# Attention steps joined into rounds of 512 keys, in a kernel of three transformer layers

## The reference, cut to what matters

```python
# layer 1: differential attention (4 heads, 2 maps each) and NSA (8 heads, 3 branches)
a = p[:, :, 0] - lam * p[:, :, 1]          # p: causal softmax of q.k, head width 64
o_diff = einsum(a, v)                       # v is 128 wide, then rms_norm of each head
pc = masked_softmax(q.kc); ps = ...(q.ks); pw = ...(q.kw)
o_nsa = g0 * (pc @ vc) + g1 * (ps @ vs) + g2 * (pw @ vw)
x = x + rms_norm(concat(o_diff, o_nsa) @ w_out); x = x + rms_norm(swiglu(rms_norm(x)))
# layer 2: short convolution and forgetting attention (8 heads)
s = q.k * scale + (c[t] - c[s]);  s = where(causal, s, -inf)   # c: running sum of log f
y_b = softmax(s) @ v
x = x + rms_norm(concat(y_a, y_b) @ w_out); x = x + rms_norm(swiglu(...))
# layer 3: conformer convolution, then the same
```

## Time and profile before

| | |
|---|---|
| median of 3 runs | 1925.96 us (1925.32 to 1926.47) |
| profiled execution | 1925.33 us, of which the span from first to last instruction 1923.5 us |
| PE busy | 1882.1 us, 98% of the span |
| PEld, DVE, ACT, POOL busy | 79%, 42%, 23%, 64% |
| mean granted TensorE clock | 0.988 of full |
| DMA | 168.29 MB, 87 GB/s |

### The profile page before, as it was taken

The page is one execution under the profiler, slowest core; times in us unless marked ns, Lnnn a source line. Parts: engine busy times, 40 slices in busy tenths (PEclk is TensorE's granted clock), DMA queues, the critical chain, the costliest instruction groups (busy, mean ns, idle before and its releaser), DMA issues.

```text
span 1923.5 us, 25700 instructions
## 1 busy us (share of the span) xinstructions
PE 1882.1 (98%) x9410; PEld 1510.2 (79%) x9410; DVE 814.2 (42%) x1397; ACT 437.0 (23%) x902; POOL 1238.6 (64%) x747
## 2 busy tenths in 40 slices
PE   8999999999999999999999999999999999999997
PEld 6776668888888898766878888889787888888886
DVE  5266563643332035154543334004993464334103
ACT  3335672311110022032311111003334331111000
POOL 7964655866666658563786667556657586666662
PEclk9999999999999999999999999999999999999998
DMA  5430102223233214211233333221323223333311
GB/s 206 121 92 30 34 23 77 84 91 98 88 117 106 82 55 144 87 56 44 77 110 94 91 98 116 95 84 50 108 73 99 77 88 90 96 98 108 106 61 44
DMA packets 44879, 168.29 MB, mean 87 GB/s; under 512 B 4984, under 2 KB 7288, under 8 KB 44672
## 3 DMA queue, kind: packets, MB, share of 16 engines
q1 hardware_dynamic: 44496, 164.56, 27.5%
q10 hardware_dynamic: 304, 2.64, 0.4%
HBM read 165.07 MB, written 2.11 MB: 87 GB/s over the span
## 4 chain that ended last, share of the span: by engine, by line
PE 88%; POOL 4%; DVE 4%; issue 2%; ACT 0%; DMA 0%; POOLq 0%; SPq 0%; DVEq 0%
PE psum L554 27%; PE psum L555 26%; PE psum L556 26%; POOL w_lo L443 2%; PE psum L747 2%; PE psum L760 1%; DVE h_lo L1484 1%; DVE tmp L1526 1%; POOL w_hi L440 1%; PE psum L783 1%; PE psum L604 1%; PE psum L851 1%; PE psum L872 1%; POOL x L464 1%; PE psum L612 1%
## 5 line engine op out<-in xcount | busy, mean ns | idle before, releaser
L443 POOL TENSOR_TENSOR w_lo<-raw,w_hi 128x1024 fp32r<-128x1024 f32 (+1 forms) x286 | 748.4, 2617 | 23.8
L554 PE MATMUL psum<-h_hi,w_hi 128*128 128x512 f32 (+1 forms) x1744 | 669.3, 384 | 15.9 <-POOL w_lo L443 9.6
L555 PE MATMUL psum<-h_lo,w_hi 128*128 128x512 f32 (+1 forms) x1744 | 658.3, 377 | 0.0
L556 PE MATMUL psum<-h_hi,w_lo 128*128 128x512 f32 (+1 forms) x1744 | 658.0, 377 | 0.0
L440 POOL TENSOR_SCALAR w_hi<-raw 128x1024 fp32r<-128x1024 f32 (+1 forms) x286 | 322.2, 1127 | 472.5 <-PE psum L556 448.5
L554 PEld LDWEIGHTS psum<-h_hi,w_hi 128*128 128x128 f32 x1744 | 328.6, 188 | 93.6 <-issue 20.8
L556 PEld LDWEIGHTS psum<-h_hi,w_lo 128*128 128x128 f32 x1744 | 327.8, 188 | 67.9
L555 PEld LDWEIGHTS psum<-h_lo,w_hi 128*128 128x128 f32 x1744 | 328.3, 188 | 63.8 <-issue 0.2
L554 PE MATMUL psum<-g_hi,w_hi 128*128 128x512 f32 (+1 forms) x594 | 219.3, 369 | 0.0
L555 PE MATMUL psum<-g_lo,w_hi 128*128 128x512 f32 (+1 forms) x594 | 218.8, 368 | 0.0
L556 PE MATMUL psum<-g_hi,w_lo 128*128 128x512 f32 (+1 forms) x594 | 218.7, 368 | 0.0
(11 more groups left out here) (281 smaller groups left out, 1912.3 us busy)
## 6 DMA issues: line engine op xcount, KB each, us to landing
raw<-in_wide SPq DMA_DIRECT2D x239, 512.0 KB, 3.6
raw<-in_down SPq DMA_DIRECT2D x48, 704.0 KB, 4.0
decay<-decay_rows ACTq DMA_DIRECT2D x1, 2048.0 KB, 7.8
out<-x SPq DMA_DIRECT2D x16, 128.0 KB, 1.7
x<-in_xt SPq DMA_DIRECT2D x3, 512.0 KB, 6.9
x<-in_xt ACTq DMA_DIRECT2D x1, 512.0 KB, 4.5
angles<-in_angles SPq DMA_DIRECT2D x1, 512.0 KB, 10.3
cols<-in_cols SPq DMA_DIRECT2D x1, 221.0 KB, 4.3
```

The costliest lines, as they stand in the source:

```text
L443: nc.gpsimd.tensor_tensor(w_lo[:, slot, 0:w], raw[:, j % RAW, 0:w], w_hi[:, slot, 0:w].bitcast(F32), ALU.subtract).then_inc(units_split, 1)
L554: pe.matmul(out_ap, lhs[0], rhs[0], start=first, stop=False)
L555: pe.matmul(out_ap, lhs[0], rhs[1], start=False, stop=False)
L556: return pe.matmul(out_ap, lhs[1], rhs[0], start=False, stop=last)
```

## The change

- `A_ROUNDS` replaces `STEPS`, `FOX_ROUNDS` replaces `FOX_STEPS`. A round holds one or two steps that lie side by side in the banks: i = 3 alone (512 keys), i = 0 beside i = 2 (128 + 384), and i = 1 beside another i = 1 (256 + 256, of the other branch in NSA, of the next pair in layer 2; alone in the differential attention). Layer 1 has 32 rounds (20 NSA, 12 differential), layer 2 has 10.
- On PE a round t is now turn(t-2), scores(t), mix(t-3). Before it was scores(t), turn(t-3), mix(t-4).
- DVE copies its half of every NSA and layer 2 round, at the head of its round, and it computes the coefficients of round t at the end of round t, one reciprocal and one product for both steps. Before it did this for step t-1 behind the maxima of step t.
- In layer 2 the masks are written first and the scores added to them.
- The weaving: 28 rounds in the eight units of layer 1, four (or two) to a unit; in layer 2 two rounds in each of the first four units and one in each of the last five. POOL now weighs all rounds of a unit before the next split.
- The read of a finished bank in layer 2 moves: `FOX_ENDS` lets ACT and DVE read both banks of two pairs at round r + 4, while PE's mix(5), the first of the third pair, is in round 8, which is just that round.
- In the token compression `low_tokens(1)` moves ahead of the second rotary embedding.

```diff
-STEPS = nsa_steps(0) + nsa_steps(1) + diff_steps(0) + nsa_steps(2) + diff_steps(1) + nsa_steps(3, (1,)) + diff_steps(2) + nsa_steps(3, (2,)) + diff_steps(3)
+def diff_rounds(head):
+    return [[("diff", head, 0, 3)], [("diff", head, 0, 0), ("diff", head, 0, 2)], [("diff", head, 0, 1)]]
+def nsa_rounds(head):
+    return [[("nsa", head, 1, 3)], [("nsa", head, 2, 3)], [("nsa", head, 1, 0), ("nsa", head, 1, 2)],
+            [("nsa", head, 2, 0), ("nsa", head, 2, 2)], [("nsa", head, 1, 1), ("nsa", head, 2, 1)]]
+A_ROUNDS = nsa_rounds(0) + nsa_rounds(1) + diff_rounds(0) + nsa_rounds(2) + diff_rounds(1) + nsa_rounds(3)[:3] + diff_rounds(2) \
+    + nsa_rounds(3)[3:] + diff_rounds(3)
-A_WEAVE = [(3, 5, 6, 7)] + [(1, 3, 4, 6, 7)] * 3 + [(1, 2, 3, 5, 6, 7)] * 3 + [(1, 3, 4, 6, 7)]
-PAIR_TURN, PAIR_MIX = 3, 4
+A_WEAVE = [(5, 7)] + [(1, 3, 5, 7)] * 6 + [(3, 7)]
+ROUND_TURN, ROUND_MIX = 2, 3
...
-WEAVE = [(3, 7)] * 3 + [(2, 5, 7)] + [(3, 7)] * 4 + [(2, 5, 7)]
+FOX_ROUNDS = [r for c in (0, 2) for r in ([(c, 3)], [(c, 0), (c, 2)], [(c + 1, 3)], [(c + 1, 0), (c + 1, 2)], [(c, 1), (c + 1, 1)])]
+FOX_ENDS = (4, 9)
+WEAVE = [(3, 7)] * 4 + [(5,)] * 5
...
+            def pair_round(t, low_start):
+                if 0 <= t - ROUND_TURN < len(A_ROUNDS):
+                    pair_turn(t - ROUND_TURN)
+                if t < len(A_ROUNDS):
+                    pair_scores(t)
+                if 0 <= t - ROUND_MIX < len(A_ROUNDS):
+                    pair_mix(t - ROUND_MIX, low_start)
...
+            def fox_mix(r):
+                steps = FOX_ROUNDS[r]
+                fox_copied(r + 1)
+                if r in (5, 7):
+                    pe.wait_ge(h_low, n.base["h_low"] + (1 if r == 5 else 2))
...
             rope("kc", place_vc)
             add_positions(0)
             add_positions(1)
-            rope("nq0", lambda: low_tokens(0))
-            rope("nq1", lambda: low_tokens(1))
-            for name in ("nq2", "nq3", "ks"):
+            rope_parts("nq0")
+            low_tokens(0)
+            low_tokens(1)
+            rope_sum("nq0")
+            for name in ("nq1", "nq2", "nq3", "ks"):
                 rope(name)
```

More of the change, by code:

```diff
@@ new lines, with places @@
+SET_BEGINS = {key: min(r for r, steps in enumerate(A_ROUNDS) if steps[0][:2] == key) for key in MIX_BANK}
+SET_ENDS = sorted((max(r for r, steps in enumerate(A_ROUNDS) if steps[0][:2] == key),) + key for key in MIX_BANK)
+A_WEAVE = [(5, 7)] + [(1, 3, 5, 7)] * 6 + [(3, 7)]
+A_WOVEN_ROUNDS = [[sum(map(len, A_WEAVE[:j])) + k for k in range(len(A_WEAVE[j]))] for j in range(len(A_WOVEN))]
+A_LEFT = sum(map(len, A_WEAVE))
+ROUND_TURN, ROUND_MIX = 2, 3
+def places(steps):
+    return [sum(step[-1] + 1 for step in steps[:k]) * P for k in range(len(steps))]
@@ new lines, in width, with steps_upto, round_col, step_col @@
+def width(steps):
+    return sum(step[-1] + 1 for step in steps) * P
+def steps_upto(rounds, r):
+    return sum(map(len, rounds[:r]))
+def round_col(r):
+    kind, head, b, i = A_ROUNDS[r][0]
+    if kind == "diff":
+        return 16 * 4 + 8 * head + 2 * i
+    return 16 * head + 2 * steps_upto(nsa_rounds(head), nsa_rounds(head).index(A_ROUNDS[r]))
+def step_col(r, k):
+    return round_col(r) + (2 * k if A_ROUNDS[r][0][0] == "nsa" else 2 * (A_ROUNDS[r][k][3] - A_ROUNDS[r][0][3]))
+def combined_by_dve(r):
+    return A_ROUNDS[r][0][0] == "diff" and A_ROUNDS[r][0][3] == NB - 1
@@ L158, in done_before @@
 def done_before(kind, head):
-    place = next(j for j, end in enumerate(SET_ENDS) if end[1:] == (kind, head))
-    earlier = [end for end in SET_ENDS[:place] if MIX_BANK[end[1:]] == MIX_BANK[kind, head]]
+    earlier = [end for end in SET_ENDS if MIX_BANK[end[1:]] == MIX_BANK[kind, head] and end[0] < SET_BEGINS[kind, head]]
     return earlier[-1][1:] if earlier else None
 def copies_by_dve(upto):
-    return sum(step[0] == "nsa" and step[3] not in COPIED_BY_ACT for step in STEPS[:upto])
-FOX_STEPS = [(c, i) for c in range(4) for i in reversed(range(NB))]
@@ new lines, in pair_scores @@
+            def pair_scores(r):
+                steps = A_ROUNDS[r]
+                if r:
+                    pe.wait_ge(pair_maxed, 2 * steps_upto(A_ROUNDS, r))
+                else:
+                    pe.wait_ge(v_out, len(TOKEN_MAJOR))
+                if steps[0][0] == "diff" and steps[0][3] == NB - 1:
+                    pe.wait_ge(rope_added, ROPES.index(f"dk{steps[0][1]}") + 1)
+                for step, off in zip(steps, places(steps)):
+                    for m in range(2):
+                        mm = pe.matmul(psum[:, 2 + m, off:off + (step[3] + 1) * P], pair_query(step, m), pair_keys(step, m), start=True, stop=True)
+                mm.then_inc(pair_scored, 1)
@@ new lines, in fox_turn, with fox_scores @@
+            def fox_turn(r):
+                pe.wait_ge(fox_weighed, r + 1)
+                if r:
+                    fox_copied(r)
+                for p in range(0, width(FOX_ROUNDS[r]), P):
+                    for m in range(2):
+                        mm = pe.transpose(psum[:, 4 + m, p:p + P], e_fox[:, m, r % 4, p:p + P], ident)
+                mm.then_inc(fox_transposed, 1)
+            def fox_scores(r, first):
+                steps = FOX_ROUNDS[r]
+                if r:
+                    pe.wait_ge(fox_maxed, 2 * steps_upto(FOX_ROUNDS, r))
+                else:
+                    pe.wait_ge(evacuated, n.now("group", -1))
+                    pe.wait_ge(fox_values, NB)
+                for k, (step, off) in enumerate(zip(steps, places(steps))):
+                    diagonal = slice(off + step[1] * P, off + (step[1] + 1) * P)
+                    for m in range(2):
+                        pe.matmul(psum[:, fox_bank(first, m), diagonal], ident16[:], causal16[:], start=k == 0, stop=False, skip_group_check=True)
+                for step, off in zip(steps, places(steps)):
+                    c, i = step
@@ L870, in fox_step @@
+                mm.then_inc(fox_scored, 1)
+            def fox_mix(r):
+                steps = FOX_ROUNDS[r]
+                fox_copied(r + 1)
+                if r in (5, 7):
+                    pe.wait_ge(h_low, n.base["h_low"] + (1 if r == 5 else 2))
+                for step, off in zip(steps, places(steps)):
+                    c, i = step
                     for j in range(i + 1):
```

480 lines of the change are left out of this document (229 added, 251 removed).

## The result

The changed kernel takes 1931.24 us (median of 8 runs, 1929.01 to 1933.53) beside 1925.49 us for the kernel before (8 runs, 1921.77 to 1926.47). The ratio is 1.0033, 95% interval 1.0022 to 1.0043: slower by 5.8 us, where the prediction had 1928.5 us and called a slower kernel the second likeliest. The profiled execution took 1932.91 us (span 1931.0), so it lies 1.7 us above the median.

What follows compares the result with a forecast made beforehand. PE, busy 98% of the span, was taken as the bound. The terms -12 - 4.1 + 8 + 4.3 + 3.8 + 2.6 + 1.5 - 1.2 = +2.9 us gave 1928.5 us, range 1920 to 1937.

Steps and rivals of the forecast that it cites:

- the forecast's own case: Whole kernel: the summed terms hold, giving 1928.5 us, within 1922 to 1930; chance 0.42.
- The likeliest sign, no change: Whole kernel: same time as before had chance 0.42, slower 0.36, faster 0.22; a timing can tell 0.2%, 3.9 us.
- rivals 1 and 2: Faster, 1918 us: layer 1's predicted waits don't appear (0.22). Slower, 1938 us: DVE becomes the bound of layer 1 (0.14).
- Part 1: Layer 1 on PE: fewer, joined rounds save fixed costs beyond the columns; gain 12 us (11 to 13.5).
- Part 2: Layer 2 on PE: fixed costs fall and 0.4 us comes back at the end; gain 4.1 us (3.5 to 4.7).
- Part 3: Layer 1's woven part: PE waits for a round's chain through the other engines; loss 8 us (3 to 12).
- Part 4: Layer 1 behind the last unit: turns wait, the opening starts at E+26.0 for 21.8; loss 4.3 us (2 to 7).
- Part 5: Layer 2, round 8: the third pair's mixing waits for a bank ACT and DVE read; loss 3.8 us (3.4 to 4.2).
- Part 6: PE's clock halves behind waits: loss 2.6 us in layer 2, 1.5 more (0 to 3.4) behind layer 1's last unit.
- the third rival: Layer 1: the clock falls at two more places, 2 * 2 us more, 1932.5 us; chance 0.16.
- Part 7: Token compression: PE's 2.51 us wait for `low_tokens(1)` goes, then PE waits for POOL's splits; gain 1.2 us (0 to 3.5).
- joined steps: Rival, layer 1: joined steps no cheaper than single ones, each joint 0.3 instead of 0.05, 1932.5 us; chance 0.06.

Runs made afterwards that it cites:

- three_coef_late: `three_rounds` plus, in layer 1, DVE's coefficients of round t - 1 behind the maxima of round t and POOL weighing a unit's last round with the next unit's: 1916.69 us.
- three_rounds: The changed kernel, but in layer 1 the turn stands three rounds behind the scores and the mixing four, instead of 2 and 3: 1925.78 us.
- two_coef_late: The changed kernel with its two rounds between scores and turn, but layer 1's coefficients of round t - 1 behind the maxima of round t: 1968.00 us.
- tail_weighed_first: The changed kernel, but POOL weighs rounds 26 to 31 of layer 1 before output-projection splits 35 and 36: 1938.03 us.
- both_mended: The changed kernel with layer 1's three rounds and late coefficients, as in `three_coef_late`, and layer 2's finished banks read at the head of the round: 1910.14 us.
- fox_read_first: The changed kernel, but in layer 2 ACT and DVE read the finished banks at the head of round r + 4 instead of its end: 1924.65 us.

## Why the prediction came out as it did

The time lies in the range (1920 to 1937), 2.7 us above the forecast and just outside the forecast's own case (1922 to 1930). As a change it is twice what was forecast: 5.8 us for 2.9. The likeliest sign, no change, was wrong; slower had 0.36. The range was also said to take in most of rivals 1 and 2, which it doesn't: their times, 1918 and 1938, both lie outside it. By its steps:

- **Part 1, fixed costs of layer 1: right.** An NSA round costs 0.54 us, 0.57 was predicted, and mixing behind scores costs the 0.21 us that was taken for it. `three_coef_late` is the cleanest check: its woven part of 124.2 us holds 107.8 us of columns (an estimate, all its matmuls at the prediction's times per pass) and 2.1 of idle, which leaves 14.3 for 28 rounds, and 14.6 follow from the prediction's rates. But one thing was counted twice. The gain of 12 us is that of all steps, while part 4 compared whole lengths behind the last unit, in which the fixed costs of those steps are already contained. That flattered the sum by some 1.5 us, an estimate.
- **Part 2, layer 2: right.** With the two traces' waits and half clocks taken out, the fixed costs gave 4.2 us, where 4.5 follow from the prediction's rates. The 0.4 us at the end came back as predicted: PE's wait for the fourth split of the output projection grew from 3.59 to 3.97 us. Together 3.8 us for 4.1.
- **Part 3, waits in the woven part: the chain right, the size somewhat small, one cause missed.** 10 us were predicted. With 14.3 us of fixed costs, 109.1 of columns (the same estimate) and 1.6 of half clock, the woven part of 137.2 us leaves 12. I had walked the waits through as a matter of slack between PE and the chain of a round. `three_rounds` gave the chain a whole round more and took away only 0.9 us of the drawn idle (some 2.5 us in all, by the same subtraction), while moving DVE's coefficients, with the extra round in place, removed the rest. Without the extra round the same move cost 37 us, so it takes both. The step that failed is where the prediction took DVE's wait for the exponentials, which it names, for a delay of the rotary products alone. It delays everything behind it on DVE, the copy and the maxima of the next round above all, and it grows where POOL's split holds the product.
- **Part 4, behind the last unit: right in its walk, wrong in what it left out.** turn(26), (27) and (28) start 4.6, 9.1 and 14.7 us behind E = 261.8; predicted 5.3, 9.1, 14.7. From 272.2 to 282.4 the rows run at half clock, so turn(30) starts at 25.0 for 23.2 and the opening at 28.3 for 26.0. The step that failed is that the walk was made at full clock, with a clock term that was too small.
- **Part 5: right**, 3.92 us for 3.8, and confirmed by taking it away.
- **Part 6, the clock: right in layer 2, too small in layer 1.** In layer 2 the stand drops the clock for 6.8 us, which cost 2.7 (2.6 predicted); the drop at the output projection got shorter by half, which gave 1.5 back. That was luck and not the change: with the same layer 2 it lasted 6.8 us in five of the six other kernels. In layer 1 the half clock lasted 3.4 us before, and 13.6 after: 3.4 in the start, behind waits of 0.58 and 1.83 us, and 10.2 behind the last unit. That costs about 4 us more than before, 1.5 were predicted. In this the third rival, which had 0.16, describes what happened in this trace; the drop in the start is absent from two other traces of the same code.
- **Part 7: right as far as can be told**, 1.2 predicted, 1.4 measured, with an interval that takes in no change at all.

The sum for layer 1 was +1.8 us and 6.6 were measured: 2.1 from larger waits, 2.5 from the clock, 1.5 from the double count, less 1.3 that stay unassigned (columns that now lie behind the last unit are among them). These shares are estimates from one trace of each kernel. Layer 2 was +2.3, and 1.3 were measured, 1.5 of it better by the shorter drop. As to the rivals: the first (waits don't appear) is excluded by 9.7 us of idle; DVE as the bound is excluded by `three_coef_late`, in which DVE does the same work in 124 us instead of 137 without holding PE; joined steps are as cheap as predicted. What the change lost, it lost by the places of the bank read, the coefficients and the turn, and by the half clocks behind the waits, not by joining.

The Trainium skill, TensorE: Matmul & The Clock Gate, Loop structure matters more than you think, has a long wait between matmuls make PE go cold. The runs agree for the long stand: 3.92 us were followed by half clock in all seven kernels that have it, and its removal by none in four. Shorter waits were followed by half clock in some traces and not in others (last section).

## What to carry to other kernels

Joining steps saves the fixed costs on the engine that is the bound, and it makes each link of the chain through the other engines longer at the same time, so the distance between producer and consumer has to be counted again in microseconds rather than taken over in steps. An instruction that waits for another engine belongs behind everything on its own engine that somebody else needs sooner; look for its wait in the timeline, and at what stands behind it. Before an edit that moves a result later, follow the dependence once around: if it closes on itself within one round (`two_coef_late`), its price is paid in each round, and if work is put off (`tail_weighed_first`), look for the consumer that takes several pieces at once.

## What the runs showed of the hardware that was not expected

**A product of a few elements on DVE can last until the instruction that runs on POOL ends.** In the trace of the changed kernel, DVE and POOL at the start of layer 1:

```profile
142.86 0.18 DVE L1704 RECIPROCAL inv_sum<-row_sum 128x4 f32<-128x4 f32 x1 [0.98 <-ACT e_ring L1241]
143.07 1.67 DVE L1706 TENSOR_TENSOR coef<-gates,inv_sum 128x4 f32<-128x4 f32 x1
144.66 0.68 DVE L1717 COPY t_ring<-psum 128x512 f32<-128x512 f32 x1
...
142.37 2.35 POOL L463 TENSOR_TENSOR w_lo<-raw,w_hi 128x1024 fp32r<-128x1024 f32 x1
```

The product ends at 144.74, the split at 144.72. Seven of the 32 coefficient products of this trace take 1.0 to 2.27 us instead of 0.16 to 0.22, and each begins inside an instruction with two inputs on POOL (`w_lo`, or the sum of the maps) and ends with it. The reciprocal, with one input, takes its 0.18 us beside the same split. The Trainium skill, SBUF — State Buffer, Who interferes with whom, says that a DVE instruction with two SBUF inputs contends with a GpSimd instruction that reads SBUF; the rows agree. The prediction's second rival had this mechanism, with 1.5 us a unit as the point from which it decides. It comes to about 11 us in layer 1's attention. In the kernel before it was there too: 11 of its 48 products were held, for 8 us in all, and one of them (195.31 to 195.69) inside `w_hi`, which has one input and ends at 195.68. In `both_mended` it is again 8 us. So it matters only where something that PE wants stands behind the product.

**A half clock can begin behind short waits, and need not.** In the start of layer 1 the half clock (3.4 us at 142.5) came behind two waits of 0.58 and 1.83 us with tiles between them. Waits of 0.59 and 1.82 us stand in the trace of `fox_read_first` too, whose layer 1 is the same code, and no half clock is there (its woven part is 135.4 us for 136.8, from tile to tile), nor in that of `tail_weighed_first`, with the same two waits. In the kernel before, the half clock at 267.3 came behind waits of 0.45 and 1.13 us. So 1.5 us of the profiled execution come from a drop that need not happen. The same holds for the first 50 us, whose code no edit touches, and where the half clock lasted between 3.4 and 6.8 us in various runs. What decides it was not settled.
